# Latent attention: rotary scores and the forming of queries and keys in rounded products, inputs kept in DRAM

## The chip, the core and the metric

The kernel runs on one core of a Trainium2 chip. TensorE (PE in the profile) multiplies, VectorE (DVE) and ScalarE (ACT) do most element-wise work, GpSimd (POOL) the rest, and SyncE (SP) issues DMAs; ScalarE issues some too. The metric is the device time of one execution in microseconds, as the median of several runs.

## What is computed

Two blocks follow each other on a sequence of 1024 positions with 1024 channels. The first has two hybrid layers; the change touches these alone. In such a layer the normed and shifted input `h` is projected once into the inputs of three kinds of attention and their gates:

```
proj = h @ w_in
c_q, c_kv, k_pe, na_qkv, diff_qkv, g_mla, g_na, g_diff = split(proj)
q  = (rms_norm(c_q) @ w_uq)                  # 6 heads of 64 + 32 (rotary) channels
kv = (rms_norm(c_kv) @ w_ukv)                # per head: 64 key channels, 64 value channels
k  = concat([k_nope, k_pe for every head])   # 64 + 32
q, k = rms_norm(q), rms_norm(k); the last 32 channels of each are turned (rope)
o_mla = attention(q, k, v)                   # full softmax over 1024 keys
o_na  = neighbourhood attention              # 6 heads of 64
o_d   = differential attention               # 4 heads
y = concat([o_mla * silu(g_mla), o_na * silu(g_na), o_d * silu(g_diff)]) @ w_out
x = x + gate * y
```

The second block has a state-space and stick-breaking mixer, two large multilayer perceptrons and gates; it takes the second half of the time and stays as it is.

## The kernel before

Everything is in float32. Where the kernel says "rounded product", both operands are split into a rounded part of float32r (`hi`) and the rest (`lo`), and a product is made as hi x hi + hi x lo + lo x hi: three products of one pass. A plain float32 product appears in the trace as two records of TensorE. Activations lie channel by channel: 128 partitions, 8 tiles `k`, 1024 columns (positions), worked in halves of 512 (`hf`).

A hybrid layer goes through these stages, each with its own loop on every engine, tied by semaphores; `phase_end` makes all engines meet.

1. **Projection** (`projected`, L969): 10 weight blocks of 1 MB; each group is one tile of 128 outputs for one half, 24 rounded products of 128x128 by 128x512. ScalarE rounds a weight block, VectorE (`block_rest`, L2619) makes its rest, some groups ahead. The last two groups make the shared rotary key `k_pe` (`pe`), whose 32 columns lie at the end of block 9; VectorE evicts them (L3020) and writes the small selection matrices `picks` (L3033, L3035). The normed input is in `m` (hi) and `n` (lo).
2. **Neighbourhood attention**: the regions of `m` and `n` are wanted for other things, so GpSimd first adds hi and lo into `n` again, 8 tiles (L3710). TensorE spreads the rotary key with `picks` (L1377), and 24 steps of attention follow.
3. **Differential attention**: 32 units. GpSimd makes one small factor in each (L3724), VectorE waits for it and combines two softmax maps (L3128). Meanwhile SyncE loads the latent weights `lt_wq`, `lt_wk`, `lt_wv`.
4. **Latent attention** (`latent`): three pairs of heads, 8 query tiles each, so 24 steps `s`. The queries and keys of a pair are formed in chunks of 256 columns, four of keys (kind 1) and four of queries (kind 0) per pair, 24 chunks `p` in the order `LAT_CHUNKS`. The first six are formed before step 0 (`LAT_AHEAD`), chunk p+6 in step p. A chunk goes through all engines: TensorE `latent_main` (L1049 keys, L1052 queries: float32 products of 256 columns), ScalarE squares (L1948), GpSimd their sum (L3742), TensorE column sums (L1059), ScalarE the root (L1783, L1785), VectorE scaling (L2818). The rotary part of a key is one more multiplication (L2852), that of a query a turn of four operations (`latent_turned`, L2871 to L2879); the 64 plain channels are rounded by ScalarE (`latent_high`, L1963) and VectorE makes their rest (`latent_low`, L2863).
   In step s TensorE runs in this order: scores of step s (`latent_scores`: the plain channels as rounded products, two heads in two row groups of 64, L1075; then the rotary channels as four float32 products in four row groups of 32, L1080), the main product of a chunk, transposes of the step before (`latent_probs_t`, L1092, twice), between these the values of two steps before (L1107), and the chunk's column sums. VectorE takes the maxima (L2885), copies one of two transposed maps (L2893) and the values (L2898); ScalarE takes the exponentials (L1971) and copies the other map (L1979).
   Scores wait for the chunks that they need by `LAT_NEEDS`: all keys of the pair, and the query quarter of the tile.
   During steps 6 to 21 ScalarE and GpSimd split the layer's input again for the gate products (`gate_input`, L1988 and L3748), 16 halves.
5. **Gates and output projection** (`end_part`, L1209 to L1211, rounded). The first gate group is begun in steps 24 and 25, in three parts of 2, 2 and 4 tiles.

SyncE issues its DMAs in a fixed order. A weight block waits until the block two before is used up (`streamed`); the loads for the latent phase stand ahead of the first gate block, and the second gate block waits for the reciprocals of the last head pair.

## Time and profile before

| | us |
|---|---|
| median of 3 runs | 3917.64 (3914.71 to 3918.3) |
| profiled execution | 3922.74 |
| its span in the profile | 3920.8 |
| TensorE busy | 3792.8 |
| VectorE busy | 2644.9 |
| ScalarE busy | 1928.5 |
| GpSimd busy | 667.7 |

Times in the trace are microseconds from the span's start. In layer 0 the projection ends near 264, the latent phase's scores begin at 528 and its gates at 727; layer 1 follows with the same pattern about 890 us later. The trace names the program's tensors by the region that they lie in (`arena`, `h`, `m`, `n`, `w`), so a line number tells more than a name. Where `[x <- ...]` stands behind a row of a timeline, the engine was idle for x us before it, and what follows the arrow released it.

### The profile page before, as it was taken

The page shows a single profiled execution, that of the slowest core. Times are in us where ns is not written, and L with a number is a line of the kernel's source. Part 1 is how long each engine was busy: PE and PEld are TensorE (multiplying, and loading weights), DVE is VectorE, ACT ScalarE, POOL GpSimd, SP SyncE. Part 2 cuts the span into 40 slices and gives each one's busy share as a digit, 9 for nine tenths or more (in the row PEclk, how much of TensorE's full clock was granted, in tenths as well). Part 3 has the DMA queues.
Part 4 walks back from the last instruction along what each step waited for, and adds up shares of the span by engine and source line. Part 5 has one row for each costly group of instructions (what it writes and reads, how often), then busy time and mean ns, then how long its engine had stood idle before and what let it go on. Part 6 is the DMA issues. An engine that isn't in the chain of part 4 may idle for free.

```text
span 3920.8 us, 52203 instructions
## 1 busy us (share of the span) xinstructions
PE 3792.8 (97%) x21022; PEld 2891.3 (74%) x21022; DVE 2644.9 (67%) x3273; ACT 1928.5 (49%) x2784; POOL 667.7 (17%) x731
## 2 busy tenths in 40 slices
PE   8999999999999999999999889999999999999999
PEld 6875567787875567787853568888888888888887
DVE  4436967675436967534435563889889868898898
ACT  5336865424336865424346443544545654444454
POOL 0120111101130111102048841000000340000010
PEclk9999999999999999999999999999999999999999
DMA  4112000252112000032100001111112101211111
GB/s 186 60 41 52 1 1 12 76 208 94 49 51 52 1 1 9 25 118 77 44 22 1 25 33 65 47 68 58 43 54 75 44 33 54 76 43 54 65 54 65
DMA packets 57232, 209.70 MB, mean 53 GB/s; under 512 B 14368, under 2 KB 15008, under 8 KB 44960
## 3 DMA queue, kind: packets, MB, share of 16 engines
q1 hardware_dynamic: 41648, 150.25, 10.9%
q10 hardware_dynamic: 15344, 56.11, 4.0%
q8 instruction: 168, 2.75, 0.3%
q14 instruction: 72, 0.59, 0.0%
HBM read 189.56 MB, written 12.58 MB: 52 GB/s over the span
## 4 chain that ended last, share of the span: by engine, by line
PE 87%; DVE 7%; ACT 3%; issue 2%; POOL 1%; DMA 0%; ACTq 0%; DVEq 0%; POOLq 0%
PE ps L1676 34%; PE ps L969 15%; PE ps L1385 3%; PE ps L1209 3%; PE ps L1211 3%; PE ps L1210 3%; PE ps L1075 2%; PE ps L1438 2%; PE ps L1427 2%; PE ps L1340 2%; PE ps L1326 1%; PE ps L1356 1%; PE ps L1092 1%; PE ps L1481 1%; PE ps L1080 1%
## 5 line engine op out<-in xcount | busy, mean ns | idle before, releaser
L1676 PE MATMUL ps<-x_piece1hi,w_piece1hi 128*128 128x512 f32 x672 | 262.4, 390 | 0.2 <-DVE x_piece1lo L3420 0.2
L1676 PE MATMUL ps<-x_piece0hi,w_piece0hi 128*128 128x512 f32 x672 | 262.3, 390 | 0.0
L1676 PE MATMUL ps<-x_piece0lo,w_piece0hi 128*128 128x512 f32 x672 | 261.5, 389 | 0.0
L1676 PE MATMUL ps<-x_piece0hi,w_piece0lo 128*128 128x512 f32 x672 | 261.4, 389 | 0.0
L1676 PE MATMUL ps<-x_piece2hi,w_piece2lo 128*128 128x512 f32 x672 | 261.4, 389 | 0.0
L1676 PE MATMUL ps<-x_piece1lo,w_piece1hi 128*128 128x512 f32 x672 | 261.4, 389 | 0.0
L1676 PE MATMUL ps<-x_piece1hi,w_piece1lo 128*128 128x512 f32 x672 | 261.4, 389 | 0.0
L1676 PE MATMUL ps<-x_piece2hi,w_piece2hi 128*128 128x512 f32 x672 | 261.4, 389 | 0.0
L1676 PE MATMUL ps<-x_piece2lo,w_piece2hi 128*128 128x512 f32 x672 | 261.4, 389 | 0.0
L969 PE MATMUL ps<-n_hi_m,w_lo 128*128 128x512 f32 x608 | 238.6, 392 | 0.0
L3926 POOL TENSOR_TENSOR rope_cos<-rope_cos,arena 128x512 f32<-128x512 f32 x42 | 65.5, 1559 | 735.5 <-ACT arena L2399 732.4
L2824 DVE TENSOR_REDUCE small<-ps 128x1 f32<-128x1024 f32 x128 | 154.5, 1215 | 33.5 <-PE ps L1385 33.5
L2154 ACT ACTIVATE h<-ps,small 128x1024 f32<-128x1024 f32 x128 | 142.7, 1115 | 54.7 <-DVE small L2824 54.6
L2885 DVE TENSOR_REDUCE small<-ps 128x1 f32<-128x1024 f32 x96 | 113.1, 1219 | 63.0 <-PE ps L1080 63.0
L1971 ACT ACTIVATE arena<-ps,small 128x1024 f32<-128x1024 f32 x96 | 107.0, 1114 | 98.6 <-DVE small L2885 98.6
L3926 POOL TENSOR_TENSOR rope_sin<-rope_sin,arena 128x512 f32<-128x512 f32 x28 | 45.2, 1615 | 640.7 <-ACT arena L2399 638.3
L2453 ACT ACTIVATE m<-m 128x1024 f32<-128x1024 f32 x80 | 85.0, 1062 | 132.2 <-DVE m L3464 104.2
L1676 PEld LDWEIGHTS ps<-x_piece1hi,w_piece1hi 128*128 128x128 f32 x672 | 126.2, 188 | 27.2 <-DVE x_piece1lo L3420 0.6
L1676 PEld LDWEIGHTS ps<-x_piece0hi,w_piece0hi 128*128 128x128 f32 x672 | 126.2, 188 | 26.6 <-DVE w_piece1lo L3413 0.2
L1676 PEld LDWEIGHTS ps<-x_piece0lo,w_piece0hi 128*128 128x128 f32 x672 | 126.2, 188 | 26.5 <-issue 0.5
L1676 PEld LDWEIGHTS ps<-x_piece1lo,w_piece1hi 128*128 128x128 f32 x672 | 126.2, 188 | 26.5 <-issue 0.5
L1676 PEld LDWEIGHTS ps<-x_piece1hi,w_piece1lo 128*128 128x128 f32 x672 | 126.2, 188 | 26.2
(489 smaller groups left out, 10438.5 us busy)
## 6 DMA issues: line engine op xcount, KB each, us to landing
w<-in_wstream SPq DMA_DIRECT2D x87, 1024.0 KB, 4.9
arena<-in_wstream SPq DMA_DIRECT2D x40, 1024.0 KB, 4.9
arena<-in_wstream ACTq DMA_DIRECT2D x16, 1024.0 KB, 5.2
out<-h ACTq DMA_DIRECT2D x32, 256.0 KB, 2.6
h<-in_na_bias ACTq DMA_DIRECT2D x6, 1152.0 KB, 5.6
h<-in_xT SPq DMA_DIRECT2D x2, 2048.0 KB, 17.6
m<-in_wstream SPq DMA_DIRECT2D x4, 1024.0 KB, 17.2
h<-in_xT ACTq DMA_DIRECT2D x4, 1024.0 KB, 10.4
```

What stands on the lines that cost most here:

```text
L969: last = mm(dst, a_part[:, k, wcols], b_part[:, tile0 + k, :], start=(k == 0 and b_part is hi and a_part is wb[0]), stop=(k == nk - 1 and ...
L1209: mm(dst, wb[0][:, k, wcols], hi[:, k, :], start=(k == 0), stop=False)
L1210: mm(dst, wb[0][:, k, wcols], lo[:, k, :], start=False, stop=False)
L1211: last = mm(dst, wb[1][:, k, wcols], hi[:, k, :], start=False, stop=(k == KT - 1))
L1385: last = mm(ps[:, 2 * i + hf, :], q[r0:r0 + 32, t * P:t * P + P], k[r0:r0 + 32, hf * HALF:hf * HALF + HALF], start=True, stop=True)
L1676: last = mm(dst[:, e, :], a_part[:, pair, k, f], b_part[:, k, :], start=(n in FRESH and half == 0 and k == 0 and t == 0), stop=(half == 1 ...
L1971: nc.scalar.activation(lt_p[:, u % 4, :], psf[:, 2 * j * HALF:(2 * j + 2) * HALF], ACT.Exp, bias=negm[:, u:u + 1], accum_out=sums[:, u:u + ...
L2154: nc.scalar.activation(df_p[:, 2 * (c % 3) + i, :], psf[:, 2 * i * HALF:(2 * i + 2) * HALF], ACT.Exp, bias=negm[:, e:e + 1], accum_out=sum ...
L2453: nc.scalar.activation(x, x, ACT.Square if st.kind == "up" else ACT.Sigmoid).then_inc(sems["unit_done"], 1)
L2824: V.reduce_max(negm[:, u:u + 1], src, AX.X, negate=True).then_inc(sems["m_ready"], 1)
L2885: V.reduce_max(negm[:, u:u + 1], psf[:, 2 * j * HALF:(2 * j + 2) * HALF], AX.X, negate=True)\
L3926: G.tensor_tensor(out=x, in0=x, in1=ring[:, r % 2, :], op=ALU.add).then_inc(sems["t_added"], 1)
```

## The change

Six things change in each of the two hybrid layers.

- The rotary part of the latent scores becomes three rounded products in place of one in float32, each in four row groups of 32. For this the turned queries and keys of every chunk are split: ScalarE rounds (`turned_high`), GpSimd subtracts (`turned_low`), and `latent_scores` waits for it.
- `latent_main` forms queries and keys in three rounded products each. GpSimd splits the inputs (`lt_q`, `lt_kv`) at the start of neighbourhood attention and the weights during units 4 to 10 of the differential phase (`parted`).
- The chunk order of a pair begins with the first query quarter, then the four key quarters. Before step 0 VectorE turns each query as soon as it is scaled.
- The groups of the shared rotary key hold the hi and lo weight columns side by side, so that two products per tile (by hi and by lo of the input) take the place of three; `picks` gets 32 more rows that add the two parts. VectorE copies the columns together once per layer.
- The normed input in its two parts is written to DRAM during the projection (16 DMAs of 512 KB from SyncE, two behind each of eight weight blocks) and read back during the latent phase for the gates. GpSimd's 8 additions and the 16 `gate_input` splits of ScalarE and GpSimd go.
- The gate products take the tiles in the order `GATE_K`, with tile 3 last, which is read back only when the last scores are made.

The diff, cut to its core:

```diff
-LAT_CHUNKS = [(hp, *x) for hp in range(LAT_PAIRS) for x in ((1, 0), (1, 1), (1, 2), (1, 3), (0, 0), (0, 1), (0, 2), (0, 3))]
+LAT_CHUNKS = [(hp, *x) for hp in range(LAT_PAIRS) for x in ((0, 0), (1, 0), (1, 1), (1, 2), (1, 3), (0, 1), (0, 2), (0, 3))]
 LAT_AHEAD = 6
-LAT_NEEDS = [LAT_CHUNKS.index((hp, 0, t // 2)) + 1 for hp in range(LAT_PAIRS) for t in range(NT)]
+LAT_NEEDS = [max(LAT_CHUNKS.index((hp, 0, t // 2)), LAT_CHUNKS.index((hp, 1, 3))) + 1 for hp in range(LAT_PAIRS) for t in range(NT)]
+GATE_K = (0, 1, 2, 4, 5, 6, 7, 3)
...
+            def input_save(layer, k):
+
+                sp.wait_ge(sems["x_hi"], H2 * KT * (layer + 1))
+                sp.wait_ge(sems["x_split"], H2 * KT * (layer + 1))
+                sp.wait_ge(sems["lay_split"], LAY_SPLIT * layer)
+                sp.wait_ge(sems["masks"], NA_MASKS * layer)
+                for i, x in enumerate((n_hi_m, n_lo)):
+                    sp.dma_start(saved[i, :, k, :], x[:, k, :].bitcast(F32)).then_inc(sems["restored"], 16)
+
+            def input_back(layer, tiles, parts=(0, 1), key="lay_split"):
+                sp.wait_ge(sems["restored"], 2 * 16 * KT * (layer + 1))
+                for k in tiles:
+                    for i in parts:
+                        sp.dma_start((n_hi_h, n_lo)[i][:, k, :].bitcast(F32), saved[i, :, k, :]).then_inc(sems[key], 16)
...
                 streamed(j)
+                if layer < L and 2 <= b < 2 + KT:
+                    input_save(layer, b - 2)
+                if j in DIFFERENTIAL_AT:
+                    sp.wait_ge(sems["lat_ready"], LAT_C * (layer + 1))
+                    input_back(layer, (0, 1, 4, 5, 6, 7))
+                    input_back(layer, (2,), (1,))
+                    sp.wait_ge(sems["o_full"], (NA_STEPS + DF_STEPS + LAT_STEPS) * (layer + 1) - LAT_STEPS + LAT_AT_LAST + 1)
+                    input_back(layer, (2,), (0,))
+                    sp.wait_ge(sems["s_full"], (NA_STEPS + 2 * DF_U + LAT_STEPS) * (layer + 1))
+                    input_back(layer, (3,), key="masks")
...
+                        if g.kind == "pe":
+                            for k in range(KT):
+                                both = pe_home[:, PE_AT + 64 * k - 64:PE_AT + 64 * k + 64]
+                                for x in (hi, n_lo):
+                                    last = mm(ps[:, i % 4, :], both, x[:, k, g.hf * HALF:g.hf * HALF + HALF],
+                                              start=(k == 0 and x is hi), stop=(k == KT - 1 and x is n_lo))
+                            last.then_inc(sems["acc_ready"], g.inc)
...
-                if kind:
-                    last = mm(ps[:, bank, 0:LAT_W], lt_wk[:, hp, :], lt_kv[:, cols], start=True, stop=True)
+                for i, (a_part, b_part) in enumerate(LT_TERMS if kind else ()):
+                    last = mm(ps[:, bank, 0:LAT_W], lt_wk_parts[a_part][:, hp, :], lt_kv_parts[b_part][:, cols], start=(i == 0), stop=(i == 2))
                 for part in range(0 if kind else 2):
                     for k in range(2):
-                        last = mm(ps[:, bank, part * LAT_W:part * LAT_W + LAT_W], lt_wq[:, 2 * hp + k, part * P:part * P + P],
-                                  lt_q[:, k, cols], start=(k == 0), stop=(k == 1))
+                        for i, (a_part, b_part) in enumerate(LT_TERMS):
+                            last = mm(ps[:, bank, part * LAT_W:part * LAT_W + LAT_W],
+                                      lt_wq_parts[a_part][:, 2 * hp + k, part * P:part * P + P], lt_q_parts[b_part][:, k, cols],
+                                      start=(k == 0 and i == 0), stop=(k == 1 and i == 2))
...
+                pe.wait_ge(sems["lat_key_done"], LAT_KEYS * layer + 2 + LAT_NEEDS[s])
...
-                for j in range(2):
-                    for hf in range(H2):
-                        r = slice(64 * j + 32 * hf, 64 * j + 32 * hf + 32)
-                        last = mm(ps[:, 2 * j + hf, :], lt_of(hp, 1, q, r), lt_of(hp, 3, slice(hf * HALF, hf * HALF + HALF), r),
-                                  start=False, stop=True)
+                for part, (a_part, b_part) in enumerate(((1, 1), (1, 2), (2, 1))):
+                    for j in range(2):
+                        for hf in range(H2):
+                            r = slice(64 * j + 32 * hf, 64 * j + 32 * hf + 32)
+                            keys = slice(hf * HALF, hf * HALF + HALF)
+                            last = mm(ps[:, 2 * j + hf, :], lt_turned(hp, 0, q, r)[a_part], lt_turned(hp, 1, keys, r)[b_part],
+                                      start=False, stop=(part == 2))
...
+                pe.wait_ge(sems["masks"], NA_MASKS * (layer + 1))
...
+            def turned_high(layer, p):
+
+                hp, kind, quarter = LAT_CHUNKS[p]
+                x, hi, _ = lt_turned(hp, kind, slice(quarter * LAT_W, quarter * LAT_W + LAT_W))
+                act.wait_ge(sems["lat_ready"], LAT_C * layer + p + 1)
+                nc.scalar.activation(hi, x, ACT.Copy).then_inc(sems["lat_key"], 1)
...
                 latent_high(layer, LAT_AHEAD - 1)
+                for p in range(LAT_AHEAD - 1):
+                    turned_high(layer, p)
...
                         latent_pt(layer, 2 * s - 1)
-                    for u in LAT_GATE_AT.get(s, ()):
-                        gate_input(layer, u)
+                    if s == 0 or s - 1 in LAT_AT:
+                        turned_high(layer, LAT_AT[s - 1] if s else LAT_AHEAD - 1)
...
+                if pe_columns:
+                    dve.wait_ge(sems["v_link"], T.next("v_link"))
+                    both = home[s][:, PE_AT:PE_AT + 64 * KT].rearrange("p (k n) -> p k n", k=KT)
+                    for i, part in enumerate((home[s], w_lo[s])):
+                        from_ = part[:, 0:KT * (KVL + MLA_ROPE)].rearrange("p (k n) -> p k n", k=KT)[:, :, KVL:]
+                        last = V.tensor_copy(both[:, :, 32 * i:32 * i + 32], from_.bitcast(F32))
+                    last.then_inc(sems["w_split"], 1)
...
-                latent_turned(layer, LAT_AHEAD - 2, 0)
-                latent_turned(layer, LAT_AHEAD - 2, 1)
+                    if LAT_CHUNKS[p][1] == 0:
+                        latent_turned(layer, p, 0)
+                        latent_turned(layer, p, 1)
...
+                    V.tensor_copy(picks[MLA_QK:P, 1, :].rearrange("p (j n) -> p j n", j=4),
+                                  ident[MLA_QK:P, MLA_QK:P].unsqueeze(1).to_broadcast([P - MLA_QK, 4, MLA_ROPE]))
...
-                for k in RESTORED:
-                    G.tensor_tensor(out=n[:, k, :], in0=n_lo[:, k, :].bitcast(F32), in1=n_hi_m[:, k, :].bitcast(F32),
-                                    op=ALU.add).then_inc(sems["restored"], 1)
+                pool.sem_inc(sems["masks"], 1)
+
+                def parted(x, hi, lo):
+                    G.tensor_copy(hi, x).then_inc(sems["p_link"], 1)
+                    pool.wait_ge(sems["p_link"], T.next("p_link"))
+                    G.tensor_tensor(out=lo, in0=x, in1=hi.bitcast(F32), op=ALU.subtract).then_inc(sems["p_link"], 1)
+                    pool.wait_ge(sems["p_link"], T.next("p_link"))
+
+                pool.wait_ge(sems["restored"], 2 * 16 * KT * (layer + 1))
+                for k in range(2):
+                    parted(lt_q[:, k, :], *(x[:, k, :] for x in lt_q_parts))
+                parted(lt_kv, *(x[:, :] for x in lt_kv_parts))
+
...
+                    if v == 4:
+                        pool.wait_ge(sems["lat_w"], 128 * (layer + 1))
+                    if 4 <= v < 4 + 2 * LAT_PAIRS:
+                        parted(lt_wq[:, v - 4, :], *(x[:, v - 4, :] for x in lt_wq_parts))
+                    if v == 4 + 2 * LAT_PAIRS:
+                        parted(lt_wk, *(x[:, :, :] for x in lt_wk_parts))
...
+                def turned_low(p):
+                    hp, kind, quarter = LAT_CHUNKS[p]
+                    x, hi, lo = lt_turned(hp, kind, slice(quarter * LAT_W, quarter * LAT_W + LAT_W))
+                    pool.wait_ge(sems["lat_key"], LAT_KEYS * layer + 2 + p + 1)
+                    G.tensor_tensor(out=lo, in0=x, in1=hi.bitcast(F32), op=ALU.subtract).then_inc(sems["lat_key_done"], 1)
...
+                for p in range(LAT_AHEAD - 1):
+                    turned_low(p)
...
+                    if s == 0 or s - 1 in LAT_AT:
+                        turned_low(LAT_AT[s - 1] if s else LAT_AHEAD - 1)
```

## Rows read from the trace of the kernel before

**Rows 1.** Page: busy time of an engine, and the chain by line.
```profile
PE 3792.8 (97%) x21022; PEld 2891.3 (74%) x21022; DVE 2644.9 (67%) x3273; ACT 1928.5 (49%) x2784; POOL 667.7 (17%) x731
...
PE ps L1676 34%; PE ps L969 15%; PE ps L1385 3%; PE ps L1209 3%; PE ps L1211 3%; PE ps L1210 3%; PE ps L1075 2%; PE ps L1438 2%; PE ps L1427 2%; PE ps L1340 2%; PE ps L1326 1%; PE ps L1356 1%; PE ps L1092 1%; PE ps L1481 1%; PE ps L1080 1%
```

**Rows 2.** Timeline of PE, a latent step without a chunk (start, us, engine, line).
```profile
698.40 0.39 PE L1075 MATMUL ps<-w_lo,lt_high 64*128 64x512 f32 x2
698.62 0.40 PE L1075 MATMUL ps<-lt_high,w_lo 64*128 64x512 f32 x2
698.95 1.14 PE L1080 MATMUL ps<-arena 32*128 32x512 f32 x8
700.02 1.09 PE L1092 MATMUL ps<-mats,arena 128*128 128x128 f32 x8
...
703.79 1.06 PE L1092 MATMUL ps<-mats,arena 128*128 128x128 f32 x8 [0.34 <-ACT arena L1971]
...
706.37 1.14 PE L1080 MATMUL ps<-arena 32*128 32x512 f32 x8
```

**Rows 3.** Timeline of DVE in the same step.
```profile
700.16 2.36 DVE L2885 TENSOR_REDUCE small<-ps 128x1 f32<-128x1024 f32 x2 [3.14 <-PE ps L1080]
```

**Rows 4.** Timeline of PE, a step with a query chunk.
```profile
580.21 1.99 PE L1052 MATMUL ps<-arena,h 128*128 128x256 f32 x8
582.04 1.04 PE L1092 MATMUL ps<-mats,arena 128*128 128x128 f32 x8
...
584.90 1.09 PE L1092 MATMUL ps<-mats,arena 128*128 128x128 f32 x8
```

**Rows 5.** Timeline of PE, a step with a key chunk.
```profile
572.35 0.70 PE L1049 MATMUL ps<-arena,h 128*128 128x256 f32 x2
...
576.12 1.06 PE L1092 MATMUL ps<-mats,arena 128*128 128x128 f32 x8 [0.30 <-DVE arena L2893]
```

**Rows 6.** Instructions of line 1080: min/median/max ns, first and last start.
```profile
L1080 PE MATMUL ps<-arena x384: 587/640/692, 529.9 to 1610.8; 32*128 32x512 f32 x192
```

**Rows 7.** Critical chain, the last projection group; timeline of DVE behind it.
```profile
257.60 5.58 PE ps L969 x24
...
264.07 0.22 DVE L3035 COPY h<-mats 96x128 f32<-96x128 f32 x1
```

**Rows 8.** Timelines of PE and ACT at the start of the latent phase.
```profile
528.33 0.50 PE L1075 MATMUL ps<-lt_high 64*128 64x512 f32 x2
...
527.81 0.42 ACT L1963 ACTIVATE lt_high<-w 128x256 fp32r<-128x256 f32 x1 [1.73 <-DVE w L2818]
```

**Rows 9.** Timelines of PE and ACT before step 8.
```profile
596.52 0.50 PE L1075 MATMUL ps<-lt_high 64*128 64x512 f32 x2 [1.26 <-DVE arena L2879]
...
596.95 0.62 ACT L1988 ACTIVATE n_hi_h<-n 128x512 fp32r<-128x512 f32 x1
```

**Rows 10.** Timeline of POOL, additions of 256 columns.
```profile
514.40 1.41 POOL L3742 TENSOR_TENSOR h<-h,m 128x256 f32<-128x256 f32 x2 [1.82 <-ACT h L1948]
...
584.84 0.73 POOL L3742 TENSOR_TENSOR h<-h 128x256 f32<-128x256 f32 x1 [8.51 <-ACT h L1948]
```

**Rows 11.** DMA issues (count, size of each, us to landing); PE at the gate.
```profile
h<-out ACTq DMA_DIRECT2D x4, 1024.0 KB, 11.8
...
727.29 0.50 PE L1209 MATMUL ps<-n_hi_h,w_hi 128*128 128x512 f32 x1 [0.17 <-DVE w_lo L2627]
...
735.96 0.50 PE L1209 MATMUL ps<-n_hi_h,w_hi 128*128 128x512 f32 x1
```

**Rows 12.** Stretches: busy time by engine, PEclk, DMA; a wait of PE.
```profile
372.00:376.00 4.00, 1.46 (x10) 0.35 (x6) 3.61 (x4) 2.40 (x4) 0.48 (x2) 0.94 0.93 228
...
388.00:392.00 4.00, 4.00 (x28) 3.34 (x28) 2.23 (x2) 2.67 (x5) 0.34 (x1) 0.50 0.02 6
921.00:925.00 4.00, 3.10 (x7) 2.48 (x8) 4.00 (x8) 0.00 (x0) 0.00 (x0) 0.58 0.41 174
...
921.90 0.77 PE L969 MATMUL ps<-n_hi_m,w_hi 128*128 128x512 f32 x1 [3.08 <-DVE n_lo L2751]
```

85 lines of the change are left out of this document (38 added, 47 removed).

## The prediction

> **What bounds the kernel now.** I read the page first: TensorE is busy for nearly the whole span, and over half of the chain that ended last lies in product lines that the diff leaves alone (L1676, L1209 to L1211, most of L969) [rows 1]. What counts is therefore the time in three places of each of the two layers: the last groups of the projection, the start of the latent phase, and its 24 steps. For these I read the timelines by engine.
>
> In a late latent step, without a chunk, the cycle is this. The rotary scores start at 698.95, 0.33 us after the last pair of rounded scores, and hold TensorE for 1.07 us [rows 2]. Then VectorE takes two maxima, 2.36 us together [rows 3], and a copy, and only then, 3.77 us after the scores, may the second transposes start (703.79) [rows 2]. Both score parts lie in that cycle, so a shorter rotary part shortens every such step. In a step with a query chunk the next transposes follow at 584.90, 4.69 us after the scores, which is more than those 3.77: TensorE bounds it, with 0.9 us of cover gone before VectorE would [rows 4]. In a step with a key chunk the second transposes wait 0.30 us for VectorE's copy, again 3.77 us after the scores: a shorter key product gives nothing there [rows 5].
>
> **Rotary scores, 48 steps.** Two records stand for one full-precision product, so 384 records are 48 steps of four products [rows 6]. They go: 0.33 + 1.07 = 1.40 us from the last pair of rounded scores to the next work [rows 2]. Twelve rounded ones come, in three rounds of four, each round in four row groups and four banks. A pair of rounded products in two row groups takes 0.22 to 0.23 us (698.40 to 698.62) [rows 2]; the old rotary part shows that four row groups run abreast, since eight records of 0.64 us end within 1.14. So a round should cost 0.23. Entry stays at 0.33 and the last round gets 0.1 for the change of tile: 0.33 + 0.23 + 0.23 + 0.33 = 1.12, a gain of 0.26 to 0.28. I take 0.26. Bounds: 0.37 if neither change of tile costs anything, and -0.3 if the rounds ran two by two. Sum: 48 x 0.26 = **-12.5 us**.
> The Trainium skill (TensorEngine Tiling (Array Packing), Key Properties) says that changing the tiling mode drains TensorE. By it neither 0.33 goes away; the row of 0.33 against 0.22 bears that out, and the bound of 0.37 is the less likely end.
>
> **Query chunks.** Four products of 256 columns take 1.83 us (580.21 to 582.04), 0.229 per record [rows 4]. Twelve rounded ones come. A rounded product of 512 columns costs 0.2325 in the projection [rows 7], the same as a two-pass record of 256, so I take half of it and 0.006 more: 12 x 0.122 = 1.46, a gain of 0.37. Ten of the twelve chunks of a layer are formed inside steps: 20 x 0.37 = **-7.4 us**. Bounds: 0.5, or a loss of 0.96 if each took as long as one of 512 columns (12 x 0.2325 = 2.79); the old record of 256 columns loaded its own 128 columns of weights in its 0.229 without showing them, so I stay near the first. Key chunks: nothing, by [rows 5]. Weights and inputs of these products are split by GpSimd: 3 splits at the start of neighbourhood attention, where 8 additions go, and 7 splits in the differential phase.
>
> **Rotary part of the projected keys.** Each of these groups, two in a layer, has 16 products instead of 24, in an unbroken run of TensorE that ends the phase: 8 x 0.2325 = 1.86, four groups, 7.4 us. Behind the last group VectorE makes two small copies and now a third, 0.2 more in each layer [rows 7]. The two strided weight copies are made some groups ahead, under groups of 5.6 us. **-7.0 us**.
>
> **The start of a latent phase.** Scores of step 0 start at 528.33, right behind TensorE's differential sums, with no wait [rows 8]. Now they also wait for five turned parts, each rounded by ScalarE and subtracted by GpSimd. ScalarE's last rounding of this stage begins at 527.81 [rows 8], and all five new ones stand behind it in its queue. With the first query ahead of the keys, VectorE has its four turning operations behind it earlier, and I put that rounding at 526.8. The first new one then ends about 527.5 and GpSimd starts 0.07 later. Its subtraction of 256 columns takes about 0.70 in a row, priced by its addition of the same size [rows 10]: five of them end at 531.1 and the scores start at 531.2, 2.9 late. Two layers: **+5.8 us** (bounds +2 and +8). Differential logs of ScalarE stand behind the five roundings too, but TensorE needs them only after the scores.
>
> **Head pairs 2 and 3, steps 8 and 16.** TensorE already waits here: 1.26 us, for the turned query [rows 9]. The query now comes four chunks earlier and that wait goes. In its place comes the last key chunk: formed in step 6, it is rounded by ScalarE only in step 7, behind root and copy, where the rounding of a gate input now starts (596.95) [rows 9]. Add 0.42 for the rounding, 0.07, 0.73 for GpSimd [rows 10] and 0.14 to TensorE: 598.3, against 596.52. So 1.8 late, four times: **+7.1 us** (bounds 0 and +10). Other steps need their quarters two steps after they are formed: no wait.
>
> **Inputs in DRAM.** The additions that restored them go, and TensorE didn't wait for these. Each save follows a weight load and is 1 MB; the next load is 24 us away. Loading back is 8 MB in a layer; four loads of 1 MB landed in 11.8 us [rows 11], so the first 7 MB need about 21 us. They may start after step 18, five steps of 7.42 us before the gate, which starts at 727.3 [rows 2, 11]. The last tile waits for the last scores, which end near 722 (3.77 us and the second transposes stand between them and the gate); its 1 MB should be there by 728, and it is read at 735.96 [rows 11]. The next weight block stands behind these waits in SyncE's queue, but it waited for the end of the last head pair anyway. Cost 0; at half that rate the gate would wait some 5 us in each layer. ScalarE and GpSimd lose 16 roundings and 16 subtractions there and gain 24 smaller ones.
>
> **GpSimd in the differential phase.** Seven splits, about 1.5 us each, run beside VectorE's combination of two maps, which has two inputs in SBUF. I allow 0.1 us each: **+1.5 us** (bounds 0 and, if each split delayed VectorE by half its length and TensorE with it, +10).
> The Trainium skill (SBUF — State Buffer, the shared port pair) says that a VectorE operation with two SBUF inputs and a GpSimd one that reads SBUF exclude each other for a whole instruction. By it alone each of the 14 splits would cost up to one GpSimd operation of 0.7 us, so +10 in all. No row read here shows such a wait.
>
> **Sum:** -12.5 - 7.4 - 7.0 + 5.8 + 7.1 + 1.5 = -12.5. The profiled execution took 3922.74 (span 3920.8), 5.1 above the median of 3917.64; its durations differ from a median run's by a thousandth, so I take the difference from the median: 3917.6 - 12.5 = **3905.1 us**.
>
> **Rivals.**
> 1. *The new waits lower the clock* (chance 0.24). TensorE would stand still for about 3 us at six places: two starts, four changes of head pair. Before the differential phase 4 us with 1.46 us of work were followed by 16 us at a granted clock of 0.50 (1.2 GHz), up to 392, although TensorE was then busy throughout; behind the wait of 3.08 us before 921.90 the clock is 0.58 in one stretch of 4 us [rows 12]. Against it: behind the wait of 1.26 us before step 8 the first score takes 0.50 us as it does at 528.33 [rows 8, 9]. A fall as before the differential phase costs half of 16 us at most; I take 7. Two falls give 3919. From three falls (+21) it is slower than before, 3926; with four, 3933.
> The Trainium skill (TensorE: Matmul & The Clock Gate, HAM oscillation) says that a wait between bursts of matmuls puts the gate back to half rate. By it more of the six would fall than not, and the time would be about 3933 or more.
> 2. *Four row groups don't run abreast in rounded form* (0.10): two by two, a round costs 0.47, the rotary part takes some 0.15 more than before: -12.5 + 12.5 + 7 = +7, 3925; with half of the rounds so, 3915.
> 3. *The new waits are short* (0.12), because the splits overlap what TensorE does anyway: without +5.8 and +7.1, 3892.
> 4. *Loads back too late, or GpSimd holds VectorE* (0.05): +25, 3930.
> 5. *The change doesn't bring what it says* (0.03): weights not hidden, so forming gains nothing: -12.5 + 7.4, 3912.5.
> The forecast has the remaining 0.46.
>
> **Numbers.** A measurement of this kernel tells about 0.2% (7.8 us) from no change. The forecast's own range is 3894 to 3913: 0.40 faster, 0.06 within. Rival 3 is faster (0.12); rival 1 gives 0.08 within and 0.16 slower; rival 2 0.08 and 0.02; rival 4 0.01 and 0.04; rival 5 0.03 within. Together 0.52 faster, 0.26 the same, 0.22 slower. The range runs from rival 3 with short waits (3891) to three falls of the clock (3926).
>
> **What would show it.** Rotary records three times as many and 1.12 us from the last pair of scores to the next work; a late step of 7.15 us where it was 7.42. Query chunks of 1.46. TensorE waiting for GpSimd before the scores of steps 0, 8 and 16, some 3 us each. A granted clock of 1 through the latent phase. Wrong would be a rotary part over 1.4, a clock of 0.50 behind those waits, or a wait for a DMA before the gate.

## The result, and the profile after

The changed kernel took 3926.28 us (median of 13 runs, 3920.63 to 3933.19) beside 3918.99 us for the kernel before on the same chip (13 runs, 3910.78 to 3920.94): 7.3 us more, a ratio of 1.0021 with a 95% interval of 1.0012 to 1.0029. It is slower, by about 0.2%. The forecast was 12.5 us less. The profiled execution took 3928.82 us, its span 3926.9.

From the page of the changed kernel: busy time of TensorE (PE), VectorE (DVE), ScalarE (ACT) and GpSimd (POOL), and the chain that ended last, by engine:

```profile
PE 3776.2 (96%) x21302; PEld 2897.3 (74%) x21302; DVE 2661.0 (68%) x3279; ACT 1925.0 (49%) x2800; POOL 661.5 (17%) x771
...
PE 79%; DVE 10%; ACT 4%; issue 3%; POOL 1%; DMA 1%; ACTq 0%; DVEq 0%; POOLq 0%
```

TensorE works 16.6 us less than in [rows 1], in a span 6.1 us longer. The work was saved; the waits around it grew by more. Where they are shows when the starts of the same instruction in both traces are compared. By the last gate products of layer 1 the changed kernel is 2.1 us behind. Another 4.0 us come between 1990 and 2330 us, where no instruction differs and the clock falls several times in either kernel. In the traces of all kernels below that stretch took between 0.2 us less and 5.8 us more than in the trace of before, with the same instructions: it is scatter. Scatter hides some of the loss as well: at the start of the differential phase, where TensorE's products are the same, the changed kernel's trace gains 2.9 us in layer 0 and 1.2 in layer 1, because the granted clock is back at 1 by 382 us where it was 0.5 up to 393 before. In layer 0 the kernels below gain up to 4.3 us there or lose up to 0.6, and the largest gain is that of experiment 11, which changes little else. What the layers do has to be read from their own rows.

A late latent step, which answers to [rows 2] (start in us, duration, engine, line, instruction):

```profile
703.35 0.39 PE L1130 MATMUL ps<-lt_high,w_lo 64*128 64x512 f32 x2
703.67 0.51 PE L1137 MATMUL ps<-lt_k_turned,lt_q_turned 32*128 32x512 f32 x4
704.01 0.41 PE L1137 MATMUL ps<-lt_high,lt_q_turned 32*128 32x512 f32 x4
704.24 0.41 PE L1137 MATMUL ps<-lt_k_turned,lt_high 32*128 32x512 f32 x4
704.58 1.09 PE L1149 MATMUL ps<-mats,arena 128*128 128x128 f32 x8
```

From the last pair of rounded scores to the next work it is 704.58 - 703.35 = 1.23 us: entry 0.32, rounds of 0.34 and 0.23, and 0.34 to leave. The four row groups do run abreast. Before it was 1.40; the forecast was 1.12. These steps take 7.23 us instead of 7.42, in both layers.

A step with a query chunk (TensorE, then ScalarE, then GpSimd), which answers to [rows 4]:

```profile
612.93 0.39 PE L1105 MATMUL ps<-lt_q_hi,lt_wq_hi 128*128 128x256 f32 x1
...
614.46 1.04 PE L1149 MATMUL ps<-mats,arena 128*128 128x128 f32 x8
...
617.32 1.09 PE L1149 MATMUL ps<-mats,arena 128*128 128x128 f32 x8
618.41 0.67 PE L1113 MATMUL ps<-h,mats_r 128*128 128x256 f32 x2
```

```profile
614.31 1.12 ACT L2037 ACTIVATE arena<-ps,small 128x1024 f32<-128x1024 f32 x1 [1.71 <-DVE small L2946]
...
615.42 0.41 ACT L2022 ACTIVATE lt_high<-w 128x256 fp32r<-128x256 f32 x1
615.72 0.37 ACT L2007 ACTIVATE h<-ps 128x256 f32<-128x256 f32 x1
615.99 1.11 ACT L2037 ACTIVATE arena<-ps,small 128x1024 f32<-128x1024 f32 x1
...
617.08 0.39 ACT L2007 ACTIVATE h<-ps 128x256 f32<-128x256 f32 x1
```

```profile
617.54 0.72 POOL L3818 TENSOR_TENSOR h<-h 128x256 f32<-128x256 f32 x1 [4.13 <-ACT h L2007]
```

The twelve rounded products take 614.46 - 612.93 = 1.53 us instead of 1.83, near the 1.46 forecast. But the column sums (618.41) now start 0.15 us behind the end of GpSimd's addition (618.26), which stands behind ScalarE's second square (617.08), and that behind two exponentials with a rounding and a square between them. In [rows 10] the same addition ended at 584.84 + 0.73 = 585.57, and the column sums followed at 585.83: that chain was a quarter of a microsecond from being the bound. The row of TensorE before:

```profile
585.83 0.60 PE L1059 MATMUL ps<-h,mats_r 128*128 128x256 f32 x2
```

The query steps from step 1 on take 8.57 to 8.65 us, most 8.64, unless a slow clock lengthens one; before, most took 8.83. That is the 0.19 of the rotary part and nothing more.

The end of head pair 1, in layer 1, on TensorE, ScalarE and GpSimd, which answers to [rows 9]:

```profile
1485.36 0.67 PE L1113 MATMUL ps<-h,mats_r 128*128 128x256 f32 x2
1489.06 0.50 PE L1130 MATMUL ps<-lt_high 64*128 64x512 f32 x2 [3.03 <-POOL lt_high L3825]
```

```profile
1479.15 0.41 ACT L2029 ACTIVATE lt_k_turned<-arena 128x256 fp32r<-128x256 f32 x1
...
1486.81 1.00 ACT L2045 ACTIVATE arena<-ps 128x1024 f32<-128x1024 f32 x1
1487.71 0.41 ACT L2029 ACTIVATE lt_k_turned<-arena 128x256 fp32r<-128x256 f32 x1
```

```profile
1488.19 0.72 POOL L3825 TENSOR_TENSOR lt_high<-arena,lt_k_turned 128x256 fp32r<-128x256 f32 x1 [2.98 <-ACT lt_k_turned L2029]
```

The rounding at 1487.71 is that of the key chunk formed in step 6, in step 7, behind root and copy. The wait is as forecast: 1.26 + 1.8, and measured 3.03. Step 7 takes 11.66 us where it was 10.16 (8.83 and a wait of 1.33). In layer 0 step 8 then took 10.12 us instead of 8.64. The stretches (busy time by engine, the last three columns PEclk, the DMA share and GB/s) show why, and show the same behind the start of that latent phase:

```profile
528.00:532.00 4.00, 2.77 (x12) 1.97 (x12) 0.00 (x0) 0.00 (x0) 1.08 (x2) 0.57 0.01 4
532.00:536.00 4.00, 4.00 (x27) 3.18 (x26) 2.21 (x2) 0.95 (x1) 0.00 (x0) 0.58 0.00 0
600.00:604.00 4.00, 3.68 (x24) 2.66 (x24) 0.00 (x0) 0.00 (x0) 0.17 (x1) 0.57 0.02 4
604.00:608.00 4.00, 4.00 (x50) 3.55 (x44) 3.46 (x3) 2.26 (x5) 0.00 (x0) 1.00 0.00 0
1489.00:1493.00 4.00, 3.94 (x36) 3.14 (x37) 1.26 (x2) 0.00 (x1) 0.00 (x0) 1.00 0.01 4
```

Behind two of the waits of some 3 us the granted clock is near 0.5 (1.2 GHz) for part of a step; behind an equal one, at 1489, it is 1.

The start of the latent phase, in layer 1, answers to [rows 8]:

```profile
1420.50 0.50 PE L1130 MATMUL ps<-lt_high 64*128 64x512 f32 x2 [2.71 <-POOL lt_high L3825]
```

From the last product of the values (L1190, before L1133) to these scores it is 19.18 us in both layers; before it was 15.34. So the start costs 3.84 us more: 2.71 for this wait, and 1.13 ahead of it.

One wait was not in the forecast. While the inputs are saved, a weight block comes late. ScalarE rounds it when it has landed, VectorE splits it, TensorE waits (ScalarE, TensorE and SyncE's queue):

```profile
80.55 1.92 ACT L1852 ACTIVATE w_hi<-w 128x2048 fp32r<-128x2048 f32 x1 [4.17 <-DMA w<-in_wstream]
```

```profile
87.72 0.47 PE L1015 MATMUL ps<-n_hi_m,w_hi 128*128 128x512 f32 x1 [1.25 <-DVE w_lo L2674]
```

```profile
74.13 0.33 SPq L869 DMA_DIRECT2D w<-in_wstream  x1
74.64 0.63 SPq L908 DMA_DIRECT2D n_saved<-n_hi_m  x1
...
86.03 0.33 SPq L869 DMA_DIRECT2D w<-in_wstream  x1
```

The load issued at 74.13 lands 6.4 us later. In the kernel before it was issued at 72.84 and the rounding began at 77.63, 4.8 us later, and TensorE didn't wait. In layer 1 the same wait is 1.59 us. These two waits are not all of it: between 79 and 227 us of the trace of before the changed kernel falls 2.0 us behind it, and in the same stretch of layer 1, from 961 to 1116 us, 2.8 us.

### The profile page after: what moved, and what is told of

The parts are those of the page before. It is cut to its first block, busy times and chain, and to the rows that moved or that the text cites. A ratio compares the mean times of both kernels' runs of the same rounds, so it can differ in the third digit from the quotient of the medians.

```text
span 3926.9 us, 52937 instructions
## 1 busy us (share of the span) xinstructions
PE 3776.2 (96%) x21302; PEld 2897.3 (74%) x21302; DVE 2661.0 (68%) x3279; ACT 1925.0 (49%) x2800; POOL 661.5 (17%) x771
## 4 chain that ended last, share of the span: by engine, by line
PE 79%; DVE 10%; ACT 4%; issue 3%; POOL 1%; DMA 1%; ACTq 0%; DVEq 0%; POOLq 0%
PE ps L1735 31%; PE ps L1015 13%; PE ps L1268 3%; PE ps L1270 3%; PE ps L1269 3%; PE ps L1444 2%; PE ps L1130 2%; PE ps L1149 2%; PE ps L1399 2%; PE ps L1385 1%; PE ps L1415 1%; PE ps L1540 1%; PE ps L1497 1%; PE ps L1164 1%; PE ps L1486 1%
## 5 line engine op out<-in xcount | busy, mean ns | idle before, releaser
L1015 PE MATMUL ps<-n_hi_m,w_lo 128*128 128x512 f32 x576 | 226.1, 393 | 0.0
L1735 PEld LDWEIGHTS ps<-x_piece2hi,w_piece2hi 128*128 128x128 f32 x672 | 126.2, 188 | 26.1
```

The costliest lines, as they stand in the source:

```text
L1015: last = mm(dst, a_part[:, k, wcols], b_part[:, tile0 + k, :], start=(k == 0 and b_part is hi and a_part is wb[0]), stop=(k == nk - 1 and ...
L1735: last = mm(dst[:, e, :], a_part[:, pair, k, f], b_part[:, k, :], start=(n in FRESH and half == 0 and k == 0 and t == 0), stop=(half == 1 ...
```

## Experiments on the four waits

All were timed beside the kernel before, whose medians there were 3917.6 to 3919.1; "less" and "more" are differences of medians to the changed kernel (3926.28), good to some 3 us, so the traces decide.

**1. The start, interleaved.**

```diff
                     if p >= 2:
                         latent_high(layer, p - 2)
-                latent_high(layer, LAT_AHEAD - 1)
-                for p in range(LAT_AHEAD - 1):
-                    turned_high(layer, p)
+                    if p >= 3:
+                        turned_high(layer, p - 3)
+                turned_high(layer, LAT_AHEAD - 2)
+                latent_high(layer, LAT_AHEAD - 1)
...
                 for p in range(LAT_AHEAD):
                     squares_sum(p)
-                for p in range(LAT_AHEAD - 1):
+                    if p >= 3:
+                        turned_low(p - 3)
+                for p in (LAT_AHEAD - 3, LAT_AHEAD - 2):
                     turned_low(p)
```

> The changed kernel, with the five roundings of turned parts on ScalarE, and their subtractions on GpSimd, put between the other work of the latent start, each three chunks behind, instead of after all of it. Theory (the new wait at the latent start costs what the trace shows): the 2.71 us for which TensorE waits for GpSimd before the scores of step 0 go in both layers, and in layer 0 the stretch at 1.2 GHz behind it (step 0 took 10.76 us there and 8.22 in layer 1) goes with it: 5.4 to 8 us less than the changed kernel, so at most 2 us above the kernel before, of which the median difference was 7.3. Rival (GpSimd beside VectorE): in the start of the latent phase a VectorE product of 256 columns took 0.96 us beside a GpSimd addition and 0.42 without one; five subtractions moved into VectorE's chain lengthen it by some 0.5 us each and give 2.7 us back: no gain.

3926.5 us, ratio 1.0021 (1.0012 to 1.0030): nothing gained. The wait before the scores is gone and yet they start 19.43 us behind the values. On VectorE, GpSimd and TensorE of its trace:

```profile
1408.19 0.43 DVE L2914 TENSOR_TENSOR arena<-arena,h 128x256 f32<-128x256 f32 x1
1408.53 0.95 DVE L2925 TENSOR_TENSOR w_lo<-w,lt_high 128x256 fp32r<-128x256 f32 x1
```

```profile
1408.19 1.01 POOL L3826 TENSOR_TENSOR lt_high<-arena,lt_q_turned 128x256 fp32r<-128x256 f32 x1 [2.36 <-ACT lt_q_turned L2029]
1409.16 0.90 POOL L3819 TENSOR_TENSOR h<-h,m 128x256 f32<-128x256 f32 x1
```

```profile
1410.21 0.67 PE L1113 MATMUL ps<-h,mats_r 128*128 128x256 f32 x2 [1.44 <-POOL h L3819]
```

VectorE's subtraction takes 0.95 us beside GpSimd's, and 0.42 alone; GpSimd's take 0.90 to 1.01 for 0.73. Both chains stretch, and the sums of squares that TensorE needs first are late. So nothing was gained, as the rival said; but the two engines in each other's way are only part of the reason. The clock falls in this stretch too, at 1412 us in layer 1, and experiment 2, with GpSimd's order kept, is still at 18.87 us: 0.56 of the 19.43 are the interleaving's.
The Trainium skill (SBUF — State Buffer, the shared port pair) says that an instruction of one of these two engines blocks the other's wholly while it holds the pair; these rows fit that, 0.95 being 0.42 and most of a GpSimd instruction.

**2. The start, GpSimd's order kept.** ScalarE's part of that edit alone.

> The changed kernel, with ScalarE's roundings of the latent start put between its other work, and GpSimd's subtractions left behind its last sum of squares. Theory: the sums of squares are no longer late (TensorE waited 1.44 and 1.06 us for them when the subtractions went between them), the scores start without a wait; from the last product of the values to the first scores 18.9 us where the changed kernel has 19.18, since the combined kernel has 18.88 with a fall of the clock to 1.2 GHz in that stretch, and 17.3 to 17.5 where the clock stays. So 0.6 us less than the changed kernel if the clock falls in both layers, 3.6 less if it stays. Rival: the wait of 2.71 us is real cost and goes whole (16.5 us in both layers, 5.4 less).

3921.23 us, ratio 1.0007 (0.9998 to 1.0016). The scores start 18.86 and 18.88 us behind the values and step 0 takes 8.20 in both layers. In TensorE's rows of layer 1 the wait is gone, and the products themselves are slow:

```profile
1410.89 0.67 PE L1113 MATMUL ps<-h,mats_r 128*128 128x256 f32 x2 [1.39 <-POOL h L3819]
...
1412.74 1.92 PE L1182 MATMUL ps<-mats,arena 128*128 128x128 f32 x8
```

Eight transposes take 1.92 us here and 1.05 in the changed kernel: the clock fell behind TensorE's waits for the chunks, before the scores instead of behind them. By the traces what was gained is the slow step 0, 1.05 us on average in each layer, and 0.3: 2.7 us in all. The start itself is as the theory had it for a clock that falls, and not at the rival's 16.5. The medians say 5.1 us less, which is more than these rows hold; the difference lies within the scatter of two medians.

**3. Key chunks turned in their own step.** `latent` of ScalarE and of GpSimd call the rounding and the subtraction of a key chunk's rotary part at the end of step s, where it is formed, not of step s + 1.

```diff
-                    if s == 0 or s - 1 in LAT_AT:
-                        turned_high(layer, LAT_AT[s - 1] if s else LAT_AHEAD - 1)
+                    for q in TURNED_AT(s):
+                        turned_high(layer, q)
```

> The changed kernel, with the rotary part of a key chunk rounded and subtracted at the end of the step that forms it, where it was done at the end of the next; query chunks as before. Theory: the rounding stood one step too late in ScalarE's queue; the four waits of 3.03 us before steps 8 and 16 go whole, and with them the slower first step behind one in layer 0 (10.12 against 8.64): steps 7 and 15 take 8.64 us instead of 11.66, and the kernel is 12 to 14 us faster than the changed one, 5 to 7 under the kernel before. Rival: the last key chunk is late anyway (sums, root and turning end in that step), and the wait shrinks only to the 1.3 us it was in the kernel before: 7 us less than the changed kernel, no difference to the kernel before.

3912.9 us, ratio 0.9983 (0.9974 to 0.9991), 13.4 less. Steps 7 and 15 take 8.57 or 8.58 us, and TensorE's scores of step 8 follow the column sums without a wait:

```profile
597.69 0.67 PE L1116 MATMUL ps<-h,mats_r 128*128 128x256 f32 x2
598.29 0.50 PE L1133 MATMUL ps<-lt_high 64*128 64x512 f32 x2
```

This one place in one queue decides the sign of the whole change: with it moved, the changed kernel is 6 us faster than the kernel before.

**4. The same waits, with TensorE kept busy.**

```diff
+                for _ in range(11 if s in (NT, 2 * NT) else 0):
+                    mm(ps[:, 0, :], blk64_r, lt_kv_parts[0][:, 0:HALF], start=True, stop=True)
                 pe.wait_ge(sems["lat_lo"], LAT_C * layer + LAT_NEEDS[s])
```

> The changed kernel, with 11 rounded products of 512 columns (2.6 us, into a score bank that is free then, overwritten by the scores) on TensorE ahead of the waits before steps 8 and 16, so that it stands still there for 0.4 us instead of 3.03. The waits keep their length. Theory (it is the standing still that lowers the clock: 12 of 20 such waits in five profiles were followed by a step 1.2 to 2.7 us longer at 1.2 GHz, none of 16 such places without the wait): steps 8 and 16 take 8.64 us in all four places, no stretch at 1.2 GHz there; against the changed kernel the time falls by what the falls cost it on average, 4 x 0.94 = 3.8 us, 3 to 4 above the kernel before. Rival (the clock falls there by chance, or for what TensorE did long before): about two of the four places show the longer step again, and the time stays at that of the changed kernel.

3922.9 us, ratio 1.0013 (1.0004 to 1.0022), 3.4 less. The steps 8 and 16 take 8.64, 8.65, 8.63 and 8.63 us. TensorE before step 8, and the two stretches around it with PEclk at 1.00:

```profile
595.93 2.91 PE L1123 MATMUL ps<-lt_kv_hi,mats_r 128*128 128x512 f32 x11
599.32 0.50 PE L1132 MATMUL ps<-lt_high 64*128 64x512 f32 x2 [0.48 <-POOL lt_high L3827]
```

```profile
596.00:600.00 4.00, 3.52 (x19) 2.67 (x19) 0.88 (x2) 2.02 (x4) 0.73 (x1) 1.00 0.00 0
600.00:604.00 4.00, 4.00 (x40) 3.22 (x37) 2.00 (x2) 0.74 (x1) 0.00 (x0) 1.00 0.01 4
```

The length of the step behind such a place, over the traces of all these kernels:

```
before steps 8 and 16                    places  slow steps  cost of one, us
TensorE stands still for about 3 us        24        14       1.2 to 2.7, mean 1.5
no wait (experiments 3, 6, 9, 10)          20         0
wait as long, TensorE kept busy             4         0
```

With 14 in 24, four places in a row without a fall have a chance of 0.42^4 = 0.03 if they are independent. In the same trace the two waits of 2.71 us before step 0, which were left alone, were both followed by a slow step (9.51 and 9.53 us where 8.2 is usual). So it is the standing still that lowers the clock, as far as four places can show it.

**5. Saves behind the load.** `input_save` waits for the landing of the weight load ahead of it.

```diff
+                sp.wait_ge(sems[f"w_loaded{j % 2}"], 16 * (j // 2 + 1))
```

> The changed kernel, with each save of the inputs waiting in SyncE's queue until the weight load ahead of it has landed, so that the two don't share the DMA engines. Theory: the waits of 1.25 us (at 87.7) and 1.59 us (at 978.0) for VectorE's split of a weight block come from the load that landed 1.7 us later beside the save (6.4 us after its issue against 4.8); they go, 2.9 us less than the changed kernel. Rival: the loads there are late for another reason (both cores of the timing, the slot freed later), and the waits stay: no gain, or a loss if the later saves now hold something behind them.

3922.1 us, ratio 1.0007 (0.9998 to 1.0016), 4.2 less. The rounding of the block begins 4.7 us after the issue at 73.75 again, and both waits for the split of a weight block are gone:

```profile
78.47 1.92 ACT L1853 ACTIVATE w_hi<-w 128x2048 fp32r<-128x2048 f32 x1 [2.48 <-DMA w<-in_wstream]
```

Between 79 and 227 us, and in the same stretch of layer 1, this kernel keeps its distance to the kernel before within 0.1 us. So the saves cost all of the 2.0 and 2.8 us that the changed kernel loses there: 4.8 us, of which the two waits are 2.8.

## Experiments on the products

**6. Rotary scores in full precision**, the four products of before, without roundings, subtractions and their waits.

> The changed kernel, with the rotary scores in 4 full-precision products again, and without the roundings, the subtractions and the waits for them. Theory: the rotary part costs 0.19 us more in each of 48 steps (+9), and what its rounded form brought as waits goes: 4 x 3.03 before steps 8 and 16, 2 x 2.7 at the starts, and the slow steps behind them (3 to 5 us): 20 to 22 less; in all 11 to 13 us faster than the changed kernel, 3914. So the rounded rotary scores, as they were put in, cost more than they brought. Rival: the waits are those of the new chunk order (the first query ahead, the last key chunk formed last) and stay for VectorE's turned part: then it is 9 us minus at most 7, no faster than the changed kernel.

3911.98 us, ratio 0.9984 (0.9975 to 0.9992), 14.3 less. Query steps take 8.82 us, late ones 7.42; steps 7 and 15 take 8.74. From the values to the first scores it is 16.4 us in layer 1, where the clock stayed: 1.06 more than before. That is the price of the first query ahead of the keys, without any rounding. So the rotary scores, as put in, brought 9 us and cost some 23 (the 14.3 of the medians and these 9).

**7. Query chunks in full precision**, 4 products for 12.

```diff
-                        for i, (a_part, b_part) in enumerate(LT_TERMS):
-                            last = mm(...
+                        last = mm(ps[:, bank, part * LAT_W:part * LAT_W + LAT_W],
+                                  lt_wq_parts[0][:, 2 * hp + k, part * P:part * P + P].bitcast(F32),
+                                  lt_q_parts[0][:, k, cols].bitcast(F32), start=(k == 0), stop=(k == 1))
```

> The changed kernel, with the query chunks formed by 4 full-precision products instead of 12 rounded ones; the low parts are left out (it takes the rounded high parts as float32), so its output differs. Theory (ScalarE's chain bounds a query step, not TensorE): the chunk's products take 1.83 us again instead of 1.53, and the query steps stay at 8.64 to 8.75 us; over 20 of them the time is that of the changed kernel, or up to 2 us more. Rival (my forecast: TensorE bounds the query step): each query step takes 0.30 us longer, 8.94, and the kernel 6 us longer than the changed one, 13 above the kernel before.

3927.87 us, ratio 1.0025 (1.0015 to 1.0036): 1.6 more, no difference that can be told. Its query steps take 8.64 to 8.67 us, so the shorter products bring nothing.

**8. The rounding of a chunk behind both exponentials.**

```diff
-                    if s - 1 in LAT_AT:
-                        latent_high(layer, LAT_AT[s - 1])
                     if p is not None:
                         latent_squares(layer, p, 7, 0)
...
                     if p is not None and LAT_CHUNKS[p][1] == 0:
                         latent_squares(layer, p, 7, 1)
+                    if s - 1 in LAT_AT:
+                        latent_high(layer, LAT_AT[s - 1])
```

> The changed kernel, with ScalarE's rounding of the formed chunk (0.3 us in the queue) moved from between the two exponentials of a step to behind them. Theory: in a step with a query chunk the chain that ends last is VectorE's maximum, two exponentials with rounding and first square between them, the second square, GpSimd's sum of squares, TensorE's column sums, scores; that is why the shorter products of the query chunks gained nothing (8.64 us a step against 8.83, only the rotary part's 0.19). With 0.3 us taken out of that chain, the 20 query steps take 8.35 us and the kernel is 5 to 6 us faster than the changed one, 1 to 2 above the kernel before. Rival: TensorE's own order bounds the step (products of the query chunk after all, or the second transposes behind the first values), then the step stays at 8.64 and the time at that of the changed kernel.

3923.42 us, ratio 1.0016 (1.0007 to 1.0025), 2.9 less. Query steps take 8.34 us, as expected: GpSimd's addition now ends before TensorE gets to the column sums. Only half of the sum came: step 2 grew from 8.64 to 9.31, and this trace has four slow steps behind waits where the changed kernel's has two, which may be chance.

**9. All four repairs, and once more with full-precision query chunks.** Experiments 2, 3, 5 and 8 (not in step 2).

> The changed kernel with four repairs together: rotary roundings of the latent start put between ScalarE's other work (GpSimd's subtractions stay behind its last sum of squares); key chunks' rotary parts rounded in the step that forms them; the rounding of a formed chunk behind both exponentials (except in step 2, which grew from 8.64 to 9.31 us with it); each save behind its weight load. Theory: the gains add up: 13 (pairs) + 4 (saves) + 4 (exponentials, with step 2 left alone) + 5 to 7 (both starts without a wait and without a slow first step), 26 us less than the changed kernel, about 3900, ratio to the kernel before 0.995. Rival: they share the same time (clock behind one wait or another, the DVE chain at the start), then 18 to 20 less, 3907.

> The combined kernel, with the query chunks formed by 4 full-precision products again (low parts left out, as in query_full). Theory: once the rounding stands behind both exponentials, ScalarE's chain leaves 8.34 us a query step and TensorE is the next bound; the products 0.30 us longer then show, 8.6 us a step, 5 to 6 us in 20 steps more than the combined kernel. Rival: the chain still ends last and the products stay hidden: no difference to the combined kernel.

3902.45 us, ratio 0.9962 (0.9949 to 0.9974), for the combined kernel, and 3905.43, 0.9966 (0.9954 to 0.9978), with full-precision query chunks. TensorE in a query step of the combined kernel, and of the other:

```profile
614.90 1.09 PE L1153 MATMUL ps<-mats,arena 128*128 128x128 f32 x8
615.83 0.60 PE L1117 MATMUL ps<-h,mats_r 128*128 128x256 f32 x2
616.36 0.49 PE L1134 MATMUL ps<-lt_high 64*128 64x512 f32 x2
```

```profile
612.16 1.99 PE L1108 MATMUL ps<-lt_q_hi,lt_wq_hi 128*128 128x256 f32 x8
614.00 1.04 PE L1152 MATMUL ps<-mats,arena 128*128 128x128 f32 x8
```

8.35 us a query step (616.36 - 608.01) against 8.64: the 0.30 us that the rounded forming saves show once ScalarE's chain is out of the way, and not before. They show in 14 of the 20 query steps; steps 0 to 3 of a layer differ by 0.2 together, so the two traces differ by 4.6 us in the steps, and the medians by 3.0, where 5 to 6 were expected. The gain of the repairs is 24 us of the 26 expected; step 2 stayed at 9.31, because the edit had to leave out step 1, not step 2 (VectorE's subtraction of step 1 waits 0.81 us for the moved rounding, and two combinations and a turning stand behind it).

**10. The start filled.** The combined kernel, TensorE's first two differential sums in its two longest waits of the start; the rounding of a chunk at its old place in step 1.

> The combined kernel, with two more edits: TensorE's first two differential sums (3.7 us of work) go into its two longest waits of the latent start (1.28 and 0.96 us) instead of behind the chunks, and the rounding of a formed chunk keeps its old place in step 1, not in step 2. Theory: the start gets 2 to 3.7 us shorter in each layer, bounded by GpSimd's last subtraction, and its clock no longer falls; VectorE's low part in step 1 no longer waits 0.8 us and steps 1 to 3 take 25.1 us instead of 26.0. 6 to 9 us less than the combined kernel, about 3895. Rival: the chain of VectorE and GpSimd sets the start, and TensorE's sums in the gaps delay it: nothing gained there, and 2 us from steps 1 to 3.

3902.57 us, ratio 0.9955 (0.9942 to 0.9969): no difference to the combined kernel. The scores start 17.3 us behind the values instead of 18.9, but step 0 takes 9.65 and 9.79 us instead of 8.21. TensorE is done early and then stands still in one piece:

```profile
521.82 0.80 PE L1134 MATMUL ps<-lt_high 64*128 64x512 f32 x2 [3.29 <-POOL lt_high L3832]
```

```profile
520.00:524.00 4.00, 2.18 (x10) 1.94 (x12) 1.96 (x3) 1.71 (x5) 1.65 (x3) 0.50 0.00 0
```

GpSimd's last subtraction bounds the start; TensorE's work only chooses where the wait is. Steps 1 to 3 took 25.35 us instead of 25.97.

**11. The projection groups alone**, on the kernel before.

```diff
+                        if g.kind == "pe":
+                            for k in range(KT):
+                                both = pe_home[:, PE_AT + 64 * k - 64:PE_AT + 64 * k + 64]
+                                for x in (hi, n_lo):
+                                    last = mm(...
```

> The kernel before, with the change's edit of the rotary part of the projected keys alone: 16 products a group instead of 24, the wide copies of their weights, and the sum of the two halves in the picking product. Theory (the term of the forecast, -7.0): the trace of the changed kernel shows 3.6 us less in each layer from before these groups to behind them, and waits of 0.2 and 0.5 us for GpSimd ahead of them; 6 to 7 us less than the kernel before, ratio 0.9983. Rival: VectorE's strided copies hold the other splits of the weight block and give half of it back: 3 us less.

3908.43 us beside 3919.07 for the kernel before, ratio 0.9970 (0.9959 to 0.9981). In its trace they shorten layer 0 by 3.8 us and layer 1 by 5.5, of which 1.7 come from a shorter stretch at 1.2 GHz behind them; 7.6 in all, above what was expected and just inside the interval (7.4 to 16). Where the rest of the 10.6 comes from stays open: this kernel's trace has less time at 1.2 GHz in several stretches that the edit doesn't touch, and one trace can't tell that from chance. By the medians two thirds of the best gain measured here (15.2 us, experiment 9) come from this small part; the 7.6 us of its trace are half.

## Why the prediction was wrong, point by point

What each term came to, from the traces, both layers together:

```
term                                  forecast   measured
rotary scores                          -12.5      -9.1   48 x 0.19
query chunks                            -7.4       0     step 8.83 -> 8.64, all of it rotary
projection groups                       -7.0      -7.6   2 x 3.8, experiment 11
start of the latent phase               +5.8      +7.7   2 x (19.18 - 15.34)
steps 8 and 16                          +7.1      +6.8   4 x (3.02 - 1.33)
inputs in DRAM                           0        +4.8   2.0 + 2.8, experiment 5
GpSimd in the differential phase        +1.5      +0.9   0.44 + 0.50
clock behind the waits                   0        +5.7   4 x 0.90 and 2 x 1.05, on average
sum                                    -12.5      +9.2   (medians: +7.3)
```

The terms are read from several traces, the clock's as an average; the changed kernel's own trace has two slow steps behind waits, 2.5 and 1.5 us. The 1.9 us between the sum and the medians are within their scatter.

The step that failed worst is the sentence "TensorE bounds it" on the **query chunks**. I took the cover of a query step from one wait, that of the second transposes for VectorE (0.9 us). The column sums at the end of the step wait for another chain, over both exponentials, the second square and GpSimd's addition, and its end was in my own [rows 10], 0.26 us ahead of 585.83. So nothing of the 0.37 came. Experiments 7 to 9 show it from both sides: the products' length doesn't matter until that chain is shorter, and then it gives 0.30 a step.

**The clock** is the second. My rival 1 named the mechanism rightly and both its numbers wrongly: I gave a fall 7 us, from the long stretch before the differential phase, and made it rare. It came at 14 of 24 waits of 3.03 us, and cost 1.5 us each, so that such a wait is dearer by nearly a third than its length; behind the 2.7 us before step 0 it came in 8 of 12. That the rival's three falls give 3926, the measured time, is luck: the changed kernel's trace has two in these places, and they cost 4.0 us together, not 14.
The Trainium skill (TensorE: Matmul & The Clock Gate, HAM oscillation) says that a wait between bursts, where it is long enough, puts the gate back to half rate. If these waits always were, each of the six would have been followed by a slow step; the traces show it for 22 of 36.

**Inputs in DRAM** failed on a reading: "the next load is 24 us away". The first loads of a layer are 11.9 us apart, and what counts was not the next load but the one half a microsecond ahead in the queue, which a save right behind it slows (experiment 5). That their packets share the DMA engines is the likely way, and not shown by itself.

**The rotary scores** were mis-sized: the first round takes 0.34 us where I had 0.23, so a step gains 0.19 and not 0.26. The bound of -0.3, row groups two by two, was far off; rival 2 is out. Its sum was wrong too: at 0.47 a round the rotary part takes 0.33 + 3 x 0.47 + 0.10 = 1.84, not some 0.15 but 0.44 more than before, 21 us in 48 steps in place of 7.

**The start** was right in its wait (2.9 forecast, 2.71) and wrong in what lies ahead of it. I moved ScalarE's last rounding 1.0 us earlier because VectorE would be done turning; instead the first query delays everything by 1.1, since its two squares and GpSimd's sum come before TensorE's first column sums, and it waits 1.28 us there.

**Steps 8 and 16** came as argued. **GpSimd in the differential phase** came too, somewhat below the forecast. Beside a split VectorE's combination of two maps takes 1.63 to 1.71 us (2.09 beside the largest), and 1.27 elsewhere; VectorE, then GpSimd:

```profile
404.27 1.70 DVE L3188 SCALAR_TENSOR_TENSOR h<-h,small 128x1024 f32<-128x1024 f32 x1
...
420.86 1.27 DVE L3188 SCALAR_TENSOR_TENSOR h<-h,small 128x1024 f32<-128x1024 f32 x1
```

```profile
404.17 0.72 POOL L3774 TENSOR_TENSOR lt_wq_lo<-h,lt_wq_hi 128x256 fp32r<-128x256 f32 x1
```

VectorE works some 3 us longer for it in each layer, but little of that reaches TensorE: over the units with splits the changed kernel loses 0.44 us to the kernel before in layer 0 and 0.50 in layer 1, and nothing behind them; the kernel of experiment 11, without splits, loses nothing. So the prediction's "no row read here shows such a wait" held only for the rows of before.

The forecast's structure was sound, but its two largest gains were read from one wait and one duration, and two of its costs, the start and steps 8 and 16, were read as single prices where they come in pairs: a wait and the clock behind it.

## What to carry to other kernels

Before crediting a shorter instruction in a pipelined step, list every wait of that step and how far ahead its releaser ended; the nearest is the gain at most, here 0.26 us of 0.37 less the 0.15 from GpSimd's end to TensorE's start, and none of it came. When an operation is added to an in-order queue, put it in the step in which its input becomes ready: one step too late here cost 13 us and the sign of the change. And a wait of some 3 us on TensorE costs its length and, more often than not, a slow stretch behind it.

## What the runs showed of the hardware that I had not expected

- The clock answers to TensorE's standing still: 14 of 24 waits of 3.03 us and 8 of 12 of 2.7 us were followed by a step 1.2 to 2.7 us longer, none of 4 when products without any use ran there, and none of 20 places without a wait. Taking the wait of 2.71 us out of the latent start moved the fall ahead of the scores, and brought 1.3 us a layer (experiment 2); making one long wait of several short ones brought it back (experiment 10).
- VectorE's subtraction of 256 columns takes 0.42 us, and 0.95 beside one of GpSimd (0.73 alone, 0.90 to 1.01 then). In the differential phase its combination of two maps takes 1.27 us, and 1.63 to 1.71 beside one of GpSimd's splits (0.72 us); seven splits cost TensorE 0.44 and 0.50 us.
- A save of 1 MB issued 0.5 us behind a weight load of 1 MB lengthened that load from 4.8 to 6.4 us.
- A rounded product of 256 columns is issued every 0.12 us, half of one of 512 (0.23), with its weights hidden: twelve in 1.53 us with the first.
